# Computing the value projections with tokens on the partitions, without the transposes that followed

## The reference

```python
h = x @ w_in                      # all projections, and the gates
(qa, ka, va, fa, qb, kb, vb, qc, kc, vc, qd, kd, vd, gates) = split(h)
ya = forgetting_attention(qa, ka, va, log_sigmoid(fa + b_forget))
yb = banded_attention(qb, kb, vb, window 127, bias table, sinks)
yc = differential_attention(qc, kc, vc, lambda)     # two softmaxes per head
yd = dilated_attention(qd, kd, vd, 3 patterns)
merged = sum_i sigmoid(gates[i]) * (y_i @ w_branch[i])
x = layer_norm(ALPHA * x + merged @ w_out)
x = layer_norm(ALPHA * x + shared_expert(x) + routed_experts(x, top 8 of 64))
```

## Time and profile before

| what | value |
|---|---|
| median of three timed executions | 1356.58 us |
| profiled execution | 1356.58 us, of which its span 1355.0 us |
| PE busy | 1281.0 us (95%) |
| PE weight loads busy | 933.7 us (69%) |
| DVE busy | 890.0 us (66%) |
| ACT busy | 712.3 us (53%) |
| POOL busy | 388.0 us (29%) |
| bytes moved by DMA | 311.30 MB |

### The profile page before, as it was taken

How to read it: one execution, slowest core, us unless ns; L and a number is a source line. 1 busy time by engine, 2 the same in 40 slices (tenths; PEclk the granted TensorE clock), 3 DMA queues, 4 the chain that set the end, 5 groups by cost and what they waited for, 6 DMA issues and landing times.

```text
span 1355.0 us, 15040 instructions
## 1 busy us (share of the span) xinstructions
PE 1281.0 (95%) x5608; PEld 933.7 (69%) x5608; DVE 890.0 (66%) x1167; ACT 712.3 (53%) x870; POOL 388.0 (29%) x262
## 2 busy tenths in 40 slices
PE   7999999999899999987999999999999999999965
PEld 4888766666566775553677787777777777777732
DVE  4011255465756564652688888888888888888858
ACT  4333433333233220011588888888887888887710
POOL 3433322122323351144132332223232222323201
PEclk9999999999999999988999999999999999999978
DMA  4922111111111525040799999999999999999776
GB/s 157 321 82 78 59 59 59 40 58 41 59 40 59 201 78 210 17 156 20 258 378 366 378 366 375 372 373 366 373 373 361 369 367 373 374 366 365 272 317 257
DMA packets 68120, 311.30 MB, mean 230 GB/s; under 512 B 17788, under 2 KB 17916, under 8 KB 41552
## 3 DMA queue, kind: packets, MB, share of 16 engines
q1 hardware_dynamic: 48560, 276.64, 54.8%
q0 software_dynamic: 19488, 33.70, 6.6%
HBM read 305.74 MB, written 42.01 MB: 257 GB/s over the span
## 4 chain that ended last, share of the span: by engine, by line
PE 61%; DMA 25%; DVE 5%; ACT 5%; issue 3%; another core or an unknown queue 0%; POOL 0%; SPq 0%; POOLq 0%; DVEq 0%; ACTq 0%
DMA raw<-in_w_gu 23%; PE PS L655 22%; PE PS L897 8%; PE PS L760 4%; PE PS L847 4%; ACT w_hi_e L1126 4%; PE PS L698 4%; PE PS L850 3%; PE PS L844 3%; PE PS L778 3%; PE PS L731 3%; PE PS L709 2%; PE PS L829 1%; DMA parts<-y_d 1%; PE PS L878 1%
## 5 line engine op out<-in xcount | busy, mean ns | idle before, releaser
L1442 DVE TENSOR_TENSOR w_lo_e<-raw,w_hi_e 128x2048 fp32r<-128x2048 f32 x192 | 433.6, 2282 | 4.9 <-ACT w_hi_e L1126 4.8
L1126 ACT ACTIVATE w_hi_e<-raw 128x2048 fp32r<-128x2048 f32 x192 | 368.4, 1920 | 112.3 <-DMA raw<-in_w_gu 72.0
L1670 POOL DMA_INDIRECT y_d<-y_slots,tab x64 | 113.9, 1779 | 425.7 <-PE PS L916 324.4
L1622 POOL TENSOR_TENSOR w_lo<-ring,w_hi 128x1024 fp32r<-128x1024 f32 x54 | 128.4, 2379 | 292.2 <-ACT w_hi L1028 292.2
L847 PE MATMUL PS<-w_hi_e,xs_lo 128*128 128x512 f32 x512 | 144.7, 404 | 0.0
L844 PE MATMUL PS<-w_hi_e,xs_hi 128*128 128x512 f32 x512 | 143.8, 402 | 0.0
L850 PE MATMUL PS<-w_lo_e,xs_hi 128*128 128x512 f32 x512 | 138.7, 392 | 0.0
L1286 DVE CUSTOM_DVE_ANT_0 region<-PS,region 128x128 f32<-128x128 f32 (+1 forms) x64 | 30.6, 478 | 148.7 <-PE PS L698 146.7
L1071 ACT ACTIVATE region<-region,nmax 128x128 f32<-128x128 f32 (+3 forms) x80 | 43.7, 546 | 149.7 <-DVE nmax L1286 149.5
L655 PE MATMUL PS<-x_hi,w_hi 128*128 128x512 f32 x424 | 115.5, 415 | 0.0
L847 PEld LDWEIGHTS PS<-w_hi_e,xs_lo 128*128 128x128 f32 x512 | 91.7, 188 | 33.5 <-DVE xs_lo L1468 16.2
(11 more groups left out here) (177 smaller groups left out, 1853.1 us busy)
## 6 DMA issues: line engine op xcount, KB each, us to landing
raw<-in_w_gu SPq DMA_DIRECT2D x128, 1024.0 KB, 11.2
raw<-in_w_down_e SPq DMA_DIRECT2D x64, 1024.0 KB, 10.8
ring<-in_w_merge SPq DMA_DIRECT2D x32, 640.0 KB, 3.9
ring<-in_w_proj SPq DMA_DIRECT2D x22, 512.0 KB, 3.7
parts<-y_d SPq DMA_DIRECT2D x8, 1024.0 KB, 15.8
parts<-y_d SPq DMA_DIRECT2D x4, 1536.0 KB, 12.7
region<-in_w_out SPq DMA_DIRECT2D x1, 4096.0 KB, 15.1
bias_d<-bias_rows SPq DMA_DIRECT2D x3, 1280.0 KB, 12.1
```

The costliest lines, as they stand in the source:

```text
L1126: nc.scalar.activation(w_hi_e[b][:, lo:hi], raw[b][:, lo:hi], ACT.Copy).then_inc(made, 1)
L1442: nc.vector.tensor_tensor(w_lo_e[b][:, lo:hi], raw[b][:, lo:hi], w_hi_e[b][:, lo:hi].bitcast(F32), ALU.subtract).then_inc(made, 1)
L1622: nc.gpsimd.tensor_tensor(wl, w, wh.bitcast(F32), ALU.subtract).then_inc(w_lo_made, 1)
L1670: pool.indirect_dma_start(y_d, bass.IndirectOffsetOnAxis(ap=rows, axis=0), y_slots[:, b, :], None, bounds_check=last_row, oob_is_err=False ...
```

## The change

The value projections are computed by a second function, `x_product_tokens`. In it the tiles of x are the stationary operand, 128 tokens at a time, and the 128 columns of the weights stream through. The result has the tokens on the partitions at once. For each of the four groups of 128 tokens the eight tiles of features are summed, with the three products of each tile one after the other: 4·8·3 = 96 matmuls of 128 columns. PE waits for both `w_hi` and `w_lo` before the first of them. The `turn_v` entries are gone from the order with their transposes and copies; ACT copies the bank straight into `V`; the products with the values wait for `proj_out` in place of the copy of the transposes. Queries, keys and gates keep the former function.

```diff
-    order = [("proj", c) for c in range(6)] + [("turn_v", 4)]
+    order = [("proj", c) for c in range(6)]
...
-        n = proj.pop(0)
-        order += [("proj", n)] + step(s) + [("turn_v", m) for m in (5 if s == 0 else n,) if PROJ[m][0] == "v"]
+        order += [("proj", proj.pop(0))] + step(s)
...
+            def x_product_tokens(bank, n):
+
+                wh, wl = w_hi[:, n % HALVES, :, :], w_lo[:, n % HALVES, :, :]
+                pe.wait_ge(w_hi_made, n + 1)
+                pe.wait_ge(w_lo_made, n + 1)
+                for t in range(QT):
+                    to, tok = PS[:, bank, t * P:(t + 1) * P], slice(t * P, (t + 1) * P)
+                    for c in range(KT):
+                        nc.tensor.matmul(to, x_hi[:, c, tok], wh[:, c, :], start=(c == 0), stop=False)
+                        nc.tensor.matmul(to, x_hi[:, c, tok], wl[:, c, :], start=False, stop=False)
+                        mm = nc.tensor.matmul(to, x_lo[:, c, tok], wh[:, c, :], start=False, stop=(c == KT - 1))
+                return mm
...
-                    x_product(bank, n).then_inc(proj_done, 1)
+                    (x_product_tokens if PROJ[n][0] == "v" else x_product)(bank, n).then_inc(proj_done, 1)
...
-                elif kind == "turn_v":
-                    u = turn_at[kind, n]
-                    pe.wait_ge(proj_out, n + 1)
...
-                    for t in range(QT):
-                        mm = nc.tensor.transpose(PS[:, T_BANK + u % 2, t * P:(t + 1) * P],
-                                                 vT[:, V_AT[PROJ[n][1:]] % 2, t * P:(t + 1) * P], ident[:, :])
-                    mm.then_inc(turned, 1)
...
+                    pe.wait_ge(turned_out, turn_at["turn", n] + 1)
-                    pe.wait_ge(turned_out, max(turn_at["turn", n], turn_at["turn_v", need]) + 1)
+                    pe.wait_ge(proj_out, need + 1)
...
-                        nc.scalar.activation(vT[:, V_AT[br, j] % 2, :], bank, ACT.Copy).then_inc(proj_out, 1)
+                        nc.scalar.activation(V[:, :, V_AT[br, j], :], bank.rearrange("p (t n) -> p t n", t=QT),
+                                             ACT.Copy).then_inc(proj_out, 1)
...
-                    nc.scalar.activation(V[:, :, V_AT[PROJ[n][1:]], :],
-                                         PS[:, T_BANK + u % 2, :].rearrange("p (t n) -> p t n", t=QT), ACT.Copy)\
-                        .then_inc(turned_out, 1)
```

More of the change, by code:

```diff
@@ L183, in build @@
     order = order_of_work()
-    turns = [x for x in order if x[0] in ("turn", "turn_y", "turn_v")]
+    turns = [x for x in order if x[0] in ("turn", "turn_y")]
     turn_at = {x: n for n, x in enumerate(turns)}
@@ L285, in build @@
         fg = yT[0:4, :, :]
-        vT = gate
         neg_oh = gate.rearrange("p a b -> p (a b)")[0:BUCKETS, 0:640]
@@ L1080, in _ @@
                     nc.scalar.activation(probsT[:, n % 3, 0:nk], PS[:, T_BANK + u % 2, 0:nk], ACT.Copy)\
-                        .then_inc(turned_out, 1)
-                elif kind == "turn_v":
-                    u = turn_at[kind, n]
-                    act.wait_ge(turned, u + 1)
-                    nc.scalar.activation(V[:, :, V_AT[PROJ[n][1:]], :],
-                                         PS[:, T_BANK + u % 2, :].rearrange("p (t n) -> p t n", t=QT), ACT.Copy)\
                         .then_inc(turned_out, 1)
```

## The result

The changed kernel takes 1391.46 us (median of four executions, 1389.23 to 1394.93) against 1355.41 us before (1353.61 to 1356.61): the ratio is 1.0271, 95% interval 1.0249 to 1.0293. Run once more beside other kernels it took 1390.12 us against 1356.17 us, ratio 1.0246 (1.0228 to 1.0264). Forecast were 1391 us, with 1364 to 1408 us around it.

The account below looks back on a forecast made before the run. PE, busy without gaps through the value projections, was taken as the bound: 1356.58 us + 36.8 for seven dearer projections - 3.0 for transposes = 1390.4 us, rounded up for small waits to 1391 us; range 1364 to 1408 us.

Parts of the forecast that it names:

- PE alone sets the end up to 161 us: Value projection stretch: PE busy 138.00 of 138.00 us and alone in the chain of waits, so its changes move the end.
- 111 ns a pair: Value projections: each load and 128-column matmul costs 111 ns, a floor made by the load, taken from float32 rows.
- The 81 ns of the Trainium skill: Value projections: a general rule of about 81 ns per 128-column pair, giving +16.4 us for seven; the prediction preferred the trace.
- The second rival: Value projections: load partly hidden, pairs at 60 to 100 ns; at 80 ns the kernel takes 1369 us; chance 14%.
- No row of short matmuls is closer than 111 ns.: Trace of the kernel before: claimed evidence for the 111 ns floor, held against cheaper pairs.
- The fixed extra of 12 ns: Value projections: a possible fp32r surcharge on each pair, making 123 ns and 1398 us in all.
- Seven projections, +36.8 us: Value projections on PE: each goes from 5.44 to 10.69 us, 5.25 us more, seven times.
- six groups of transposes, -2.7 us: PE between projections: six removed groups of value transposes, 0.44 us each, where PE has no idle time.
- The seventh group, -0.3 us: PE at 161.66 us: last removed transposes, partly hidden by waits for ACT; -0.3 us, range 0 to -0.5.
- Copies, `w_lo`, `proj_out`: zero: ACT's copies, PE's wait for the weight split and the value products' wait for ACT's copy: priced at nothing.
- Transposes worth 3.0 us in the end: Whole kernel: removing all seven groups of value transposes was to take -3.0 us off the total time.
- The clock's half of the dear case: Value projections: clock granted at 0.50, loads some 210 ns apart, 1457 us and more; part of a 15% chance.

Follow-up runs that it names:

- the old layout: Kernel before (weights stationary, transposes kept), with each value projection streaming x in four pieces of 128 tokens, 96 pairs instead of 24: 1391.48 us, ratio 1.0256.

## Why the prediction was right

- *PE alone sets the end up to 161 us.* Right: in the changed kernel PE has no gap from 24 to 194 us, and the delay arrives whole at the transposes after the projections.
- *111 ns a pair.* Right, 111.6 ns. That the load makes the floor was carried over from float32 rows; the experiments with 64-token tiles (60 ns) and with the old layout (111 ns) show it for fp32r.
- *The 81 ns of the Trainium skill* ("TensorE: Matmul & The Clock Gate", section "Back-to-back issue gap"). Not borne out for fp32r: inside the seven value projections of the changed kernel no load starts less than 109 ns after the one before, against 81 ns. The second rival (60 to 100 ns a pair) falls by the same distances.
- *"No row of short matmuls is closer than 111 ns."* Too strong, though nothing came of it. In the timeline of the kernel before, these four transposes start after a wait of PE:

```profile
163.17 0.42 PEld L709 LDWEIGHTS PS<-ident,region 128*128 128x128 f32 x4 [0.68 <-ACT region L1071]
```

  That is (0.42 - 0.14)/3 = 93 ns; by their single starts the second load comes 60 ns after the first, the others 110 ns. Such a close pair stands at the start of a group; the floor is one of sustained rows.
- *The fixed extra of 12 ns.* Right as a fact of pairs of 256 and 512 columns (13 ns), wrong as an addition to the floor: at 128 columns it is hidden in the load, so 123 ns did not come.
- *Seven projections, +36.8 us, six groups of transposes, -2.7 us.* Forecast was a delay of 34.1 us behind the last value projection; ACT's exponential there starts 34.3 us later than in the earlier trace rows (196.18 against 161.87).
- *The seventh group, -0.3 us.* A little more: PE's next transposes start only 33.85 us later (197.05 against 163.20), so 0.46 us went, near the end of my range (0.5). The delay of 33.9 us behind it meets the forecast's 33.8.
- *Copies, `w_lo`, `proj_out`: zero.* Right; ACT's and POOL's waits are on PE.
- *Transposes worth 3.0 us in the end.* In the trace right (2.8 us behind the projections, 3.0 at the experts), in the median too large: the run without them is level with before within 1.2 us. As a term of the sum it is the mis-sized one, by 1.8 to 4.2 us, and why is open; the uncertainty of the large term's comparison (two to three us either way) hides it.
- *Rivals.* The clock's half of the dear case does occur on this chip, and it lay nearer than the prediction could see: at half the streamed columns it costs 72 us.

By the two ratios the difference is 36.7 us (33.7 to 39.7) and 33.4 us (30.9 to 35.8); the sum was 33.8. Both hold it. That the forecast of 1391 us came within half a microsecond of 1391.46 is luck beyond that: it started from 1356.58 us where the kernel before took 1355.41 in the comparison, added about 0.6 us for waits that did not come, and took off 3.0 us for transposes that the medians do not show.

## What to carry to other kernels

A pair of load and matmul costs the longer of two things: streaming its columns (in fp32r with 13 ns on top) and loading its stationary tile. In this kernel a full tile costs 111 ns; in fp32r a pair costs more than that with 256 streamed columns (120 ns) and not with 128. Changing the layout of an output to save a transpose is worth it if the streamed side stays wide: the transposes that went cost 0.44 us a group, the narrow matmuls 5.3 us a projection. Estimated from the measured prices, two value projections side by side (256 columns, 96 x 120 ns = 11.5 us) would about match what they cost before with their transposes (10.9 + 0.9 us), if having both splits ready at once cost no wait; this was not tried, and no kernel here beats the one before.

## What the hardware showed that I had not expected

- The granted clock fell to 0.50 with PE shown busy throughout: streaming 64 columns per load of 111 ns it fell within 7 us of the first such projection's start; streaming 128 it stayed 1.00 through two such projections in a row and in the whole stretch from 24 to 194 us.
- The load follows the clock: 111 ns apart at 1.00, 210 ns at 0.50, and 60 ns with half a tile at 1.00.
- One execution of the changed kernel lacked a DVE stall of about 6 us and was 10 us faster than its timed ones. Comparing two single profiles would have given +23.4 us for a change whose timed executions give 33 to 37.
